# Two parts of 304 and 240 tokens in place of two of 272 in a two-layer encoder step

## The chip, the cores and the metric

One core of one Trainium2 chip runs one program that holds the whole step. The metric is the device time of one execution in microseconds. The kernel before takes 1821.96 us (median of three runs, 1821.05 to 1822.27).

## What is computed

Inference of two layers of a hybrid encoder on 512 prompt frames and 32 frames of a running stream. The reference, cut to what matters here:

```python
a_in, a_gate, u, v, q, k, vv, g = jnp.split(x @ w_in, IN_SPLITS, axis=-1)     # 1024 -> 6656
y_a = silu(layer_norm(causal_dwconv(conv_ext, conv_w, conv_b), ...))          # width 31
y_b = gelu(u) * spatial_gate(layer_norm(gelu(v), ...), sgu_w, sgu_b)
y_c = stick_breaking attention of q, k, vv (8 heads of 64)
merged = sum(sigmoid(g_i + b_gate_i) * (y_i @ w_branch[i]) for the 3 branches)
x = layer_norm(DN_ALPHA * x + merged @ w_out, ln1_g, ln1_b)
f_gate, f_val = jnp.split(x @ w_up, 2, axis=-1)                               # 1024 -> 2 x 2816
f = gelu(causal_dwconv(ffn_ext, ffn_conv_w, ffn_conv_b)) * f_val              # width 3
x = layer_norm(DN_ALPHA * x + f @ w_down, ln2_g, ln2_b)
```

All data is float32. Returned are the new x of all 544 frames and the new rows of the caches and states.

## The kernel before

**Layout.** Features lie on the 128 partitions, the 544 tokens (512 of the prompt, then 32 of the stream) on the free axis. x is `xT[128, 8, 544]`. A matmul takes a 128x128 block of weights as its stationary operand and the tokens as its moving operand. The output bank holds 512 float32 columns, so the tokens are worked on in two parts of `HALF` = 272 columns; `dcol(h)` is the slice of part h. Part 1 holds the last 240 prompt tokens (`BP`) and the 32 of the stream.

**Precision.** Every dense product is made of three matmuls in the type float32r: a weight chunk `raw` is split into a rounded `wh` (ScalarE, `hi`, L495) and the rest `wl` (VectorE, `lo`, L961), the activations likewise into `xh` and `xl`, and `three` (L1628, L1633, L1634) issues wh·xh, wh·xl and wl·xh into one bank. Each of the three loads its own 128x128 block of weights first.

```python
first = mm(out, a, xs[0], start=start, stop=False)
mm(out, a, xs[1], start=False, stop=False)
return mm(out, b, xs[0], start=False, stop=stop)
```

**Units and chunks.** `unit(s, b, ...)` makes one output tile of 128 features for one part: 8 (or 4) times `three`. A chunk of w_in or w_up (2048 columns, 1 MB) gives four units: two feature tiles, each for part 0 (banks 0 and 1) and part 1 (banks 2 and 3). w_branch chunks are half as large. w_out (4 chunks) is worked through for part 0 and, with its chunks kept, for part 1. Per layer that makes 832 calls of `three` for w_in, 192 for w_branch, 128 for w_out, 704 for w_up and 352 for w_down, 2208 in all; half of them are of part 0 and half of part 1.

**The down projection.** `down(h)` runs four times in a layer, twice with part 0 and twice with part 1 (once for output tiles 0 to 3, once for 4 to 7). The 22 input tiles come in groups of 3, 4, 3, 4, 4, 4 (`KGROUPS`), each its own chunk of `raw`; a chunk serves four banks, so one of 4 tiles is 48 matmuls and one of 3 tiles is 36, all of one part.

**The weights' ring.** Three slots. SyncE issues the DMA of a chunk once TensorE has begun the chunk after the last user of the slot (`slot_free`), ScalarE rounds it, VectorE makes the low half, and TensorE waits for that (`lo_full`). Both engines work strictly in the order in which the program lists their instructions, so a `hi` or `lo` behind a step of a norm waits for that step.

**The norms.** `residual`, `shift_sum`, `centre`, `square_first`, `squares_open`, `last_tiles`, `square_last`, `variance`, `off_mean`, `inverse`, `norm`, `norm_out` and `low_tiles` make the LayerNorm of one part while TensorE works on the other; `shift` and `moments` are its matmuls with plain float32 operands, which go as two passes each. The squares of the last four tiles lie in `gex`, pair sums in `cbuf`. The order of all of it is written out by hand per engine. After the last matmul of the program the norm of part 1 has nothing beside it (`tail_tiles`, L1055 to L1098, `y_tile`, L534).

Of the kernel before, what the change touches and what calls it, by code (L numbers as in the profile page):

```python
# [5 lines left out]
F32 = mybir.dt.float32  # L6
# [10 lines left out]
HALF = T // 2  # L17
BP = SEQ - HALF
# [94 lines left out]
def trunk(nc, adds, x_in, win, wbr, wout, wup, wdn, par_in, bc_in, sguw_in, kc_in, vc_in, gh_in, fh_in,  # L113
          y_out, k_out, v_out, glu_out, ffn_out, sgu_out):
    with ExitStack() as ctx:
# [35 lines left out]
        st0 = sb("st0", [P, HALF])  # L151
        st1 = sb("st1", [P, HALF])
        st2 = sb("st2", [P, HALF])
# [3 lines left out]
        tmp = sb("tmp", [P, 4, HALF])  # L157
# [5 lines left out]

        gex = sb("gex", [P, 2, GEX])
        C = top[0]
        cbuf = sb("cbuf", [P, 2, GEX - 2])
# [6 lines left out]
        fhh = [sb(f"fhh{h}", [P, FT, HALF], F32R, at=F + h * 2 * FT * HALF * 4) for h in range(2)]  # L173
        fll = [sb(f"fll{h}", [P, FT, HALF], F32R, at=F + (2 * h + 1) * FT * HALF * 4) for h in range(2)]
# [11 lines left out]
        sq = sb("sq", [P, KT, HALF], at=F + 39168)  # L186
# [12 lines left out]
        sqc = [sb("sqc0", [P, CT, HALF], at=F + 90016), sb("sqc1", [P, CT, HALF], at=F + 71168)]  # L199

        cst = [st0[:, :], cbuf[:, 0, 0:HALF]]
        csd = [st1[:, :], cbuf[:, 0, HALF:2 * HALF]]
        cinv = [st2[:, :], cbuf[:, 1, 0:HALF]]
# [227 lines left out]
        def _(pool):  # L431
# [45 lines left out]
            for t in range(4, KT):  # L477
                x = xT[:, t, dcol(1)]
                g.tensor_tensor(x, x, cbuf[:, 0, 0:HALF], ALU.subtract).then_inc(tail_cent, c.up(tail_cent))
# [3 lines left out]
        def _(act):  # L483
# [19 lines left out]
            def conv_root(h):  # L503
                act.wait_ge(ln_var, c.take(ln_var))
                A(csd[h], cbank[h][:, 0:HALF], ACT.Sqrt, bias=eps[:, 0:1]).then_inc(ln_std, c.up(ln_std))

            def square_first(h):
                act.wait_ge(lx_cent, c.take(lx_cent))
                A(tmp[:, :, :], xT[:, 0:4, dcol(h)], ACT.Square).then_inc(lx_sq, c.up(lx_sq))

            def square_last(h):
                for b in range(4):
                    c.skip(acc_full[b])
                    act.wait_ge(acc_free[b], c.take(acc_free[b]))
                    A(square(b), xT[:, 4 + b, dcol(h)], ACT.Square).then_inc(lx_sq, c.up(lx_sq))

            def root(first=None):
# [3 lines left out]
                A(st2[:, :], bo[:, 0:HALF], ACT.Square).then_inc(lx_msq, c.up(lx_msq))  # L521
                act.wait_ge(lx_var, c.take(lx_var))
                A(st2[:, :], st1[:, :], ACT.Sqrt, bias=eps[:, 0:1]).then_inc(lx_std, c.up(lx_std))

            def norm_out(h, gname, bname, tiles=range(KT)):
                for t in tiles:
# [75 lines left out]
            def plain(dst, m, b, sig_to, fn=ACT.Copy):  # L602
# [3 lines left out]
                A(dst[:, m, dcol(h)], ps[b][:, 0:HALF], fn).then_inc(acc_free[b], c.up(acc_free[b]))  # L606
# [29 lines left out]
            for l in range(DEPTH):  # L636

                def gate(b, t):
                    act.wait_ge(acc_full[b], c.take(acc_full[b]))
                    A(tmp[:, t, :], ps[b][:, 0:HALF], ACT.Sigmoid).then_inc(acc_free[b], c.up(acc_free[b]))  # L640

                def two_gates(b, t):
                    for m in range(2):
                        gate(b + m, t + m)
# [11 lines left out]
                if l == 0:  # L656
                    two_gates(0, 0)
                    two_values(2)
                    two_gates(0, 2)
# [4 lines left out]
                    for b in range(4):  # L664
                        gate(b, b)
                else:
                    root()
                    hi()
                    two_gates(0, 0)
# [4 lines left out]
                    two_gates(0, 0)  # L674
                    two_gates(2, 2)
# [3 lines left out]
                    two_gates(2, 2)  # L679
# [1402 lines left out]
```

## Time and profile before

| | |
|---|---|
| median of 3 runs | 1821.96 us |
| the profiled execution's own time | 1822.0 us |
| its span, first to last instruction | 1820.3 us |
| TensorE matmul busy / weight load busy | 1804.0 us (99%) / 1761.1 us (97%) |
| VectorE, ScalarE, GpSimd busy | 1135.1 us (62%), 771.5 us (42%), 88.9 us (5%) |
| mean granted TensorE clock | 0.997 |
| mean DMA rate | 102 GB/s |

Matmuls are pipelined: each is shown from its start to the landing of its last column, so neighbours overlap, and what the engine really pays for one is the distance between two starts. Weight loads are shown on a row of their own, PEld.

### The profile page before, as it was taken

What the parts mean: (1) busy time and instruction counts of PE and PEld (TensorE: products, weight loads), DVE (VectorE), ACT (ScalarE), POOL (GpSimd) and SP (SyncE); (2) the same over time, 40 slices, a digit from 0 to 9 for tenths busy, and PEclk for the clock granted to TensorE, in tenths of its full rate; (3) what the DMA queues carried; (4) which work ended last, traced back from release to release, by engine and by line L of the source; (5) the groups of instructions that cost most, each with busy time, mean ns of one, the idle gap of its engine ahead of it and who ended that gap; (6) DMA issues with size and microseconds to landing.
All of it is one profiled execution on the core that took longest, in us unless ns stands there. A gap on an engine that the chain in (4) does not pass through costs nothing.

```text
span 1820.3 us, 32909 instructions
## 1 busy us (share of the span) xinstructions
PE 1804.0 (99%) x14362; PEld 1761.1 (97%) x14362; DVE 1135.1 (62%) x1737; ACT 771.5 (42%) x1220; POOL 88.9 (5%) x159
## 2 busy tenths in 40 slices
PE   9999999999999999999999999999999999999997
PEld 9998899999999999999999889999999999999997
DVE  5788677654764444446668886676557644445565
ACT  4245432353553444434542564333544544434343
POOL 0024000000100000000000340000001000000000
PEclk9999999999999999999999999999999999999999
DMA  4521122222222222255525211222232222223544
GB/s 169 190 95 48 36 95 70 82 93 93 95 83 78 93 93 94 68 182 174 170 85 190 75 67 36 72 88 87 82 128 70 72 91 93 93 79 99 182 160 134
DMA packets 36512, 186.02 MB, mean 102 GB/s; under 512 B 7376, under 2 KB 11728, under 8 KB 18192
## 3 DMA queue, kind: packets, MB, share of 16 engines
q1 hardware_dynamic: 34960, 178.37, 29.0%
q10 hardware_dynamic: 1408, 5.54, 0.8%
q8 instruction: 113, 1.85, 0.4%
q14 instruction: 31, 0.25, 0.0%
HBM read 176.75 MB, written 7.15 MB: 101 GB/s over the span
## 4 chain that ended last, share of the span: by engine, by line
PE 95%; DVE 3%; ACT 1%; DMA 1%; issue 0%; ACTq 0%; DVEq 0%
PE acc L1628 29%; PE acc L1633 28%; PE acc L1634 28%; PE score L1702 1%; DVE wl L961 1%; PE small L1750 1%; PE turned L1729 1%; ACT wh L495 1%; DMA raw<-wdn 1%; PE score L1633 1%; PE score L1634 1%; PE score L1628 1%; PE small L1762 1%; PE turned L1786 0%; PE score L1904 0%
## 5 line engine op out<-in xcount | busy, mean ns | idle before, releaser
L1628 PE MATMUL acc<-xh,wh 128*128 128x272 f32 x2944 | 858.7, 292 | 2.5 <-DVE xl L915 1.5
L1633 PE MATMUL acc<-xl,wh 128*128 128x272 f32 x2944 | 848.5, 288 | 0.0
L1634 PE MATMUL acc<-xh,wl 128*128 128x272 f32 x2944 | 847.5, 288 | 0.0
L1628 PEld LDWEIGHTS acc<-xh,wh 128*128 128x128 f32 x2944 | 555.3, 189 | 18.1 <-issue 13.1
L1633 PEld LDWEIGHTS acc<-xl,wh 128*128 128x128 f32 x2944 | 555.0, 189 | 0.1
L1634 PEld LDWEIGHTS acc<-xh,wl 128*128 128x128 f32 x2944 | 553.9, 188 | 0.0
L961 DVE TENSOR_TENSOR wl<-raw,wh 128x2048 fp32r<-128x2048 f32 (+2 forms) x154 | 318.4, 2068 | 204.1 <-ACT wh L495 203.3
L495 ACT ACTIVATE wh<-raw 128x2048 fp32r<-128x2048 f32 (+2 forms) x174 | 304.9, 1753 | 158.9 <-DMA raw<-wdn 112.1
L1628 PE MATMUL acc<-fhh,wh 128*128 128x272 f32 x704 | 204.9, 291 | 1.9 <-DVE wl L961 1.8
L1634 PE MATMUL acc<-fhh,wl 128*128 128x272 f32 x704 | 202.6, 288 | 0.0
L1633 PE MATMUL acc<-fll,wh 128*128 128x272 f32 x704 | 202.6, 288 | 0.0
L1164 DVE SCALAR_TENSOR_TENSOR acc<-glu,par,acc 128x574 f32<-128x574 f32 x240 | 180.8, 813 | 0.1
L1495 DVE SCALAR_TENSOR_TENSOR cbuf<-gex,par,cbuf 128x546 f32<-128x546 f32 x44 | 34.5, 784 | 197.9 <-ACT cbuf L840 197.9
L1628 PEld LDWEIGHTS acc<-fhh,wh 128*128 128x128 f32 x704 | 132.6, 188 | 3.5 <-DVE wl L961 3.1
L1633 PEld LDWEIGHTS acc<-fll,wh 128*128 128x128 f32 x704 | 132.4, 188 | 0.2
L1634 PEld LDWEIGHTS acc<-fhh,wl 128*128 128x128 f32 x704 | 132.4, 188 | 0.0
L746 ACT ACTIVATE tmp<-acc,par 128x272 f32<-128x272 f32 x96 | 46.6, 488 | 198.1 <-PE acc L1634 198.0
L1628 PE MATMUL acc<-mh,wh 128*128 128x272 f32 x256 | 74.9, 293 | 0.0
L1108 DVE TENSOR_TENSOR_SCAN keep<-keep,zero 128x128 f32<-128x128 f32 (+4 forms) x68 | 58.8, 865 | 25.5 <-POOL beta L461 16.9
L1633 PE MATMUL acc<-ml,wh 128*128 128x272 f32 x256 | 73.8, 288 | 0.0
L1634 PE MATMUL acc<-mh,wl 128*128 128x272 f32 x256 | 73.5, 287 | 0.0
L849 ACT ACTIVATE fhh<-tmp 128x272 fp32r<-128x272 f32 x88 | 35.2, 431 | 82.0 <-DVE tmp L1523 42.3
(256 smaller groups left out, 2255.8 us busy)
## 6 DMA issues: line engine op xcount, KB each, us to landing
raw<-win SPq DMA_DIRECT2D x50, 1024.0 KB, 4.9
raw<-wup SPq DMA_DIRECT2D x44, 1024.0 KB, 4.9
raw<-wdn SPq DMA_DIRECT2D x32, 1024.0 KB, 4.9
raw<-wbr SPq DMA_DIRECT2D x24, 512.0 KB, 3.6
raw<-wdn SPq DMA_DIRECT2D x16, 768.0 KB, 4.2
raw<-wout SPq DMA_DIRECT2D x8, 1024.0 KB, 4.9
v_out<-vfm ACTq DMA_DIRECT2D x2, 1088.0 KB, 9.4
k_out<-k ACTq DMA_DIRECT2D x2, 1088.0 KB, 4.7
```

The costliest lines, as they stand in the source:

```text
L495: A(wh[s][:, 0:n], raw[s][:, 0:n], ACT.Copy).then_inc(hi_full[s], c.up(hi_full[s]))
L746: A(tmp[:, b, :], ps[b][:, 0:HALF], ACT.Sigmoid, bias=col(par, PAR["b_gate"] + 8 * BRANCHES[n] + 2 * i + b % 2)).then_inc(acc_free[b], c.u ...
L849: A(row(fhh[b // 2], 2 * i + b % 2, 0, HALF), tmp[:, b, :], ACT.Copy).then_inc(f_hi, c.up(f_hi))
L961: v.tensor_tensor(wl[s][:, 0:n], raw[s][:, 0:n], wh[s][:, 0:n].bitcast(F32), ALU.subtract).then_inc(lo_full[s], c.up(lo_full[s]))
L1108: v.tensor_tensor_scan(keep[b][:, T - w:T][:, ::-1], keep[b][:, T - w:T][:, ::-1], zero[:, 0:1].broadcast_to([P, w]), 1.0, ALU.mult, ALU.a ...
L1164: v.scalar_tensor_tensor(out=acc[:, m, :], in0=glu_at(m, j), scalar=w, in1=acc[:, m, :], op0=ALU.mult, op1=ALU.add).then_inc(vec, c.up(vec))
L1495: v.scalar_tensor_tensor(out=cbuf[:, m, :], in0=gex[:, m, 1:GEX - 1], scalar=col(par, PAR["fw"] + FT + t), in1=cbuf[:, m, :], op0=ALU.mult ...
L1628: first = mm(out, a, xs[0], start=start, stop=False)
L1633: mm(out, a, xs[1], start=False, stop=False)
L1634: return mm(out, b, xs[0], start=False, stop=stop)
L1702: mm(bs[b][:, 0:w], q[rows, ht, i * P:w], k[rows, ht, 0:w], start=True, stop=True).then_inc(s_full[b], c.up(s_full[b]))
L1729: last = pe.transpose(bt[:, kb * P:(kb + 1) * P], beta[n % 2][part][:, kb * P:(kb + 1) * P], ident[:, :])
```

## The change

The parts become 304 and 240 tokens in every stage. Instructions, their order, their number, their waits and the DMAs stay the same; only widths and addresses differ. Part 1 now holds 208 prompt tokens and the 32 of the stream. Buffers of one part's width get the wider one, and the squares and pair sums get places of their own in the room of `gex` and `cbuf`.

```diff
-HALF = T // 2
-BP = SEQ - HALF
+N0, N1 = 304, 240
+PART = (N0, N1)
+WIDE = max(PART)
+BP = SEQ - N0
...
-        st0 = sb("st0", [P, HALF])
+        st0 = sb("st0", [P, WIDE])
...
-        tmp = sb("tmp", [P, 4, HALF])
+        tmp = sb("tmp", [P, 4, WIDE])
...
-        fhh = [sb(f"fhh{h}", [P, FT, HALF], F32R, at=F + h * 2 * FT * HALF * 4) for h in range(2)]
+        f_at = (0, 2 * FT * N0 * 4)
+        fhh = [sb(f"fhh{h}", [P, FT, PART[h]], F32R, at=F + f_at[h]) for h in range(2)]
...
+        squared = [sb(f"squared{b}", [P, WIDE], at=G + o * 4) for b, o in enumerate((8, 552, 856, 1160))]
+        pair = sb("pair", [P, 2, WIDE], at=G + 1464 * 4)
...
         def dcol(h):
-            return slice(h * HALF, (h + 1) * HALF)
-        def square(b):
-            return gex[:, b // 2, 4 + b % 2 * HALF:4 + (b % 2 + 1) * HALF]
+            return slice(h * N0, N0 + h * N1)
+        def square(b, h):
+            return squared[b][:, 0:PART[h]]
...
-                v.tensor_tensor(cbuf[:, 0:2, 0:HALF], x[:, 0:2], x[:, 2:4], ALU.add).then_inc(vec, c.up(vec))
+                v.tensor_tensor(pair[:, :, 0:PART[h]], x[:, 0:2], x[:, 2:4], ALU.add).then_inc(vec, c.up(vec))
...
+                part = b // 2 if h is None else h
                 for t in range(nk):
-                    last = three((spare or ps[b])[:, 0:HALF], s, t * 256 + m * P, [x[:, t, dcol(b // 2 if h is None else h)] for x in xs],
+                    last = three((spare or ps[b])[:, 0:PART[part]], s, t * 256 + m * P, [x[:, t, dcol(part)] for x in xs],
...
-                                last = three(ps[b][:, 0:HALF], s, t * 512 + b * P,
+                                last = three(ps[b][:, 0:PART[h]], s, t * 512 + b * P,
```

Every other operation on one part (gates, products, norms, the loads of x and the stores of y) changes its width in the same way.

## Rows read from the trace of the kernel before

**Rows 1.** The page: span, busy time of the engines, granted clock in 40 slices.
```profile
span 1820.3 us, 32909 instructions
PE 1804.0 (99%) x14362; PEld 1761.1 (97%) x14362; DVE 1135.1 (62%) x1737; ACT 771.5 (42%) x1220; POOL 88.9 (5%) x159
PEclk9999999999999999999999999999999999999999
```

**Rows 2.** The page: the chain that ended last, shares by engine.
```profile
PE 95%; DVE 3%; ACT 1%; DMA 1%; issue 0%; ACTq 0%; DVEq 0%
```

**Rows 3.** Groups by line and form, PE: count, busy us, mean ns, idle before.
```profile
L1628 PE MATMUL acc<-xh,wh 128*128 128x272 f32 x2944 | 858.7, 292 | 2.5 <-DVE xl L915 1.5 <-DVE wl L961 1.0
L1628 PE MATMUL acc<-fhh,wh 128*128 128x272 f32 x704 | 204.9, 291 | 1.9 <-DVE wl L961 1.8
```

**Rows 4.** Busy time by stretch: us, PE busy (count), PEld, DVE, ACT, POOL, clock.
```profile
600.00:700.00 100.00, 100.00 (x800) 100.00 (x799) 45.52 (x94) 40.31 (x68) 0.00 (x0) 1.00 0.24 85
```

**Rows 5.** One line's instructions: duration ns min/median/max, first and last start, forms.
```profile
L1628 PE MATMUL acc<-xh,wh x2944: 282/288/576, 7.3 to 1671.0; 128*128 128x272 f32 x197
L1667 PE MATMUL small<-st,mean_c x16: 390/392/392, 472.9 to 1783.9; 128*128 128x272 f32 x16
L1714 PE MATMUL score<-sfuture,identr x4: 283/283/284, 194.4 to 1099.2; 128*128 128x32 f32 x4
```

**Rows 6.** Timeline, matmuls and weight loads at 272 us: start, us, instruction, count.
```profile
272.36 0.28 PE L1634 MATMUL acc<-xh,wl 128*128 128x272 f32 x1
272.57 0.96 PEld L1896 LDWEIGHTS turned<-wsgu,ntok 32*128 32x128 f32 x8
272.57 1.07 PE L1896 MATMUL turned<-wsgu,ntok 32*128 32x32 f32 x8
273.57 1.19 PEld L1904 LDWEIGHTS score<-wsgu,ntok 128*128 128x128 f32 x10
```

**Rows 7.** Waits of PE, longest first: us in total, times, longest.
```profile
PE acc L1628 <- DVE wl L961: 2.8, 7, 0.6
```

**Rows 8.** The page: DMA issues of w_down's chunks, us from issue to landing.
```profile
raw<-wdn SPq DMA_DIRECT2D x32, 1024.0 KB, 4.9
```

**Rows 9.** Timelines of ACT, DVE and PE in the last layer's down projection.
```profile
1739.28 1.90 ACT L495 ACTIVATE wh<-raw 128x2048 fp32r<-128x2048 f32 x1
1741.21 2.29 DVE L961 TENSOR_TENSOR wl<-raw,wh 128x2048 fp32r<-128x2048 f32 x1 [0.93 <-ACT wh L495]
1743.56 0.39 PE L1628 MATMUL acc<-fhh,wh 128*128 128x272 f32 x1 [0.61 <-DVE wl L961]
...
1788.76 1.28 DVE L1011 TENSOR_TENSOR xT<-xT,small 128x1088 f32<-128x1088 f32 x1
1790.08 1.11 ACT L509 ACTIVATE tmp<-xT 128x1088 f32<-128x1088 f32 x1 [4.75 <-DVE xT L1011]
1791.10 1.90 ACT L495 ACTIVATE wh<-raw 128x2048 fp32r<-128x2048 f32 x1
1793.03 2.29 DVE L961 TENSOR_TENSOR wl<-raw,wh 128x2048 fp32r<-128x2048 f32 x1 [2.99 <-ACT wh L495]
1795.38 0.39 PE L1628 MATMUL acc<-fhh,wh 128*128 128x272 f32 x1 [0.56 <-DVE wl L961]
```

**Rows 10.** Timeline of the tail after the last matmul of a product.
```profile
1807.73 0.44 DVE L1055 TENSOR_TENSOR xT<-xT,acc 128x272 f32<-128x272 f32 x1 [0.24 <-PE acc L1634]
1809.41 0.73 DVE L1077 TENSOR_TENSOR xT<-xT,cbuf 128x544 f32<-128x544 f32 x1 [0.77 <-ACT cbuf L901]
1811.26 1.84 DVE L1081 RECIPROCAL st<-st 128x272 f32<-128x272 f32 x1
1813.99 3.48 ACT L534 ACTIVATE xT<-sq,par 128x272 f32<-128x272 f32 x6 [2.95 <-DVE sq L1086]
```

**Rows 11.** Timeline of the head: the low half of a piece of x.
```profile
9.68 0.73 DVE L915 TENSOR_TENSOR xl<-xT,xh 128x544 fp32r<-128x544 f32 x1
```

More of the change, by code:

```diff
@@ L162, in trunk @@
         rs = sb("rs", [P, 2, 5])
+        G = top[0]
         gex = sb("gex", [P, 2, GEX])
         C = top[0]
+        assert C == G + 2 * GEX * 4
         cbuf = sb("cbuf", [P, 2, GEX - 2])
@@ L172, in trunk @@
         wl.append(sb("wl3", [P, CHUNK], F32R, at=F + 71168))
-        fhh = [sb(f"fhh{h}", [P, FT, HALF], F32R, at=F + h * 2 * FT * HALF * 4) for h in range(2)]
-        fll = [sb(f"fll{h}", [P, FT, HALF], F32R, at=F + (2 * h + 1) * FT * HALF * 4) for h in range(2)]
+        f_at = (0, 2 * FT * N0 * 4)
+        fhh = [sb(f"fhh{h}", [P, FT, PART[h]], F32R, at=F + f_at[h]) for h in range(2)]
+        fll = [sb(f"fll{h}", [P, FT, PART[h]], F32R, at=F + f_at[h] + FT * PART[h] * 4) for h in range(2)]
         yb = [sb(n, [P, CT, T], F32R, at=F + i * T4) for i, n in enumerate(("ybh", "ybl"))]
@@ L198, in trunk @@
         att = [sb("att0", [P, 5 * P], at=S), sb("att1", [P, 5 * P], at=M)]
[L199 to L203, printed above, removed]
+        sqc = [sb("sqc0", [P, CT, N0], at=F + 90016), sb("sqc1", [P, CT, N1], at=F + 71168)]
+        cst = [st0[:, 0:N0], cbuf[:, 0, 0:N1]]
+        csd = [st1[:, 0:N0], cbuf[:, 0, N1:2 * N1]]
+        cinv = [st2[:, 0:N0], cbuf[:, 1, 0:N1]]
+        squared = [sb(f"squared{b}", [P, WIDE], at=G + o * 4) for b, o in enumerate((8, 552, 856, 1160))]
+        pair = sb("pair", [P, 2, WIDE], at=G + 1464 * 4)
+        assert 552 >= GEX + 2 and 8 + WIDE <= GEX and 1464 + 2 * WIDE <= 2 * GEX + 2 * (GEX - 2)
         ps = [ctx.enter_context(nc.psum_tensor(f"acc{b}", [P, 512], F32)) for b in range(4)]
@@ L478, in _ @@
                 x = xT[:, t, dcol(1)]
-                g.tensor_tensor(x, x, cbuf[:, 0, 0:HALF], ALU.subtract).then_inc(tail_cent, c.up(tail_cent))
+                g.tensor_tensor(x, x, pair[:, 0, 0:N1], ALU.subtract).then_inc(tail_cent, c.up(tail_cent))
         @block.scalar
@@ L514, in square_last, with root @@
                     act.wait_ge(acc_free[b], c.take(acc_free[b]))
-                    A(square(b), xT[:, 4 + b, dcol(h)], ACT.Square).then_inc(lx_sq, c.up(lx_sq))
-            def root(first=None):
+                    A(square(b, h), xT[:, 4 + b, dcol(h)], ACT.Square).then_inc(lx_sq, c.up(lx_sq))
+            def root(h, first=None):
                 act.wait_ge(lx_mean, c.take(lx_mean))
@@ L673, in _ @@
                     taken(2)
-                    two_gates(0, 0)
-                    two_gates(2, 2)
+                    two_gates(0, 0, 0)
+                    two_gates(2, 2, 1)
                     hi()
@@ L885, in _ @@
                 his(3)
-                root()
+                root(0)
                 his(2)
@@ L900, in _ @@
                 hi()
-            root(lambda: A(cbuf[:, 0, 0:HALF], bo[:, 0:HALF], ACT.Copy).then_inc(mean_copied, 1))
+            root(1, lambda: A(pair[:, 0, 0:N1], bo[:, 0:N1], ACT.Copy).then_inc(mean_copied, 1))
             for t in (0, 2, 3, 4, 6, 7):
@@ L1596, in _ @@
             dve.wait_ge(mean_copied, 1)
-            off_mean(1, 0, cbuf[:, 0, 0:HALF])
-            variance()
-            off_mean(1, 1, cbuf[:, 0, 0:HALF])
-            inverse()
+            off_mean(1, 0, pair[:, 0])
+            variance(1)
+            off_mean(1, 1, pair[:, 0])
+            inverse(1)
             for p in range(4):
@@ L1677, in conv_means @@
                     pe.wait_ge(ln_sum, c.take(ln_sum))
-                    mm(cbank[h][:, 0:HALF], mean_c[:, :], cst[h], start=True, stop=True).then_inc(ln_mean, c.up(ln_mean))
+                    mm(cbank[h][:, 0:PART[h]], mean_c[:, :], cst[h], start=True, stop=True).then_inc(ln_mean, c.up(ln_mean))
             def conv_vars():
@@ L1682, in conv_vars @@
                     pe.wait_ge(ln_ssum, c.take(ln_ssum))
-                    mm(cbank[h][:, 0:HALF], mean_c[:, :], cst[h], start=True, stop=True).then_inc(ln_var, c.up(ln_var))
+                    mm(cbank[h][:, 0:PART[h]], mean_c[:, :], cst[h], start=True, stop=True).then_inc(ln_var, c.up(ln_var))
             qk_out = {}
@@ L1814, in _ @@
                         for b in range(2):
-                            last = three(ps[b][:, 0:HALF], s0, t * 256 + b * P, [x[:, t, dcol(0)] for x in xs],
+                            last = three(ps[b][:, 0:N0], s0, t * 256 + b * P, [x[:, t, dcol(0)] for x in xs],
                                          t == 0, t == KT - 1)
```

211 lines of the change are left out of this document (105 added, 106 removed).

## The prediction

> **What bounds the kernel now.** I read the page first: matmuls are in flight 99% of a span of 1820.3 us, VectorE is busy 62%, ScalarE 42%, and the granted clock is full in all 40 slices [rows 1], which is the 2.4 GHz level. The chain that ended last runs through PE for 95% of the span [rows 2]. So the time is a number of matmuls times the distance between two starts, plus the few places where PE waits. By form [rows 3] nearly everything is 272 columns wide and PE hardly sat idle before them. The code gives the count: 2208 calls of `three` in a layer, so 3 x 2208 x 2 = 13,248 matmuls, 6624 of each part.
>
> The distance comes from the table of stretches: 800 matmuls touch 100 us of the up projection [rows 4]. Each counts over its own 0.288 us [rows 5], so it is (100 + 0.29)/800 = 125.4 ns. 13,248 x 0.1254 = 1661 us of 1820. The question is what these 125.4 ns are made of: columns, or the weight load that goes beside each.
>
> **The price of a column.** 272 columns at 2.4 GHz are 113.3 ns. The float32 passes (L1667) take two clocks a column, 226.7 ns, and last 392 ns from start to landing, so the way through the array is 392 - 227 = 165 ns. The float32r matmuls last 288 ns [rows 5]; less 165 that is 123 ns in which 272 columns stream, and 2.4 ns between two streams make the 125.4. They stream 8% slower than the clock allows. This isn't the next weight load's doing: the matmul at 272.36 lasts 0.28 too, and the next load starts only at 272.57, behind its stream [rows 6]. I take the 123 ns as proportional to columns: 304 cost 137.5 + 2.4 = 139.9 ns, 240 cost 108.5 + 2.4 = 110.9 ns, together 250.8 as before. If the excess were fixed per matmul they would be 138.7 and 112.1, the same sum. A straight line gives nothing and costs nothing here, and I see no term that bends down.
>
> **The price of a load.** The eight matmuls of L1896 have 32 columns, so their loads set the pace: 0.96 us for eight, less one load's 0.19, over seven is 110 ns. The ten loads of L1904 give (1.19 - 0.19)/9 = 111 ns [rows 6]. A load can't be had faster than about 111 ns, and a narrow matmul needs 110.9. Before, the load was hidden with 14 ns to spare; now the two tie. With equal means the later one sets each step: the durations of float32r matmuls scatter from 282 ns up around 288 [rows 5], some +-3 ns usually. Taking the larger of 111.5 and a value scattering by 2.5 about 111 gives some 112.4. **+1.5 ns x 6624 = +9.9 us.** Bounds: 0 if the load hides at 108 or so (the tie never bites), +5 ns (+33 us) if load and stream disturb each other's start at a tie. I take 1.5, nearest to the load rows, measured at that pace.
>
> The Trainium skill ("TensorE: Matmul & The Clock Gate", sections "LDWEIGHTS (loading the stationary operand)" and "Back-to-back issue gap") gives a load P/1.2, so 107 ns for 128 columns, and a matmul N/2.4 + 2.5 ns. By it the narrow part would be paced by its loads at 106.7 instead of 102.5, the wide one would take 129.2, the pair 4.3 ns more than 2 x 115.8, and an estimate from that page is +28 us. The trace has 125.4 where that rule has 115.8, so I go by the rows.
>
> **Weights in `down`.** A part is one operand of a whole chunk there. With part 1 a chunk of four input tiles takes 48 x 0.1124 = 5.4 instead of 6.0 us, one of three tiles 4.05 instead of 4.5; with part 0 they take 6.7 and 5.0. The weights come at the same pace: 4.9 us to land [rows 8], 1.9 rounding, 2.3 low half [rows 9], 9.1 in all, while two chunks run. Two chunks are now 10.5 or 12.0 us; with part 1 they are 9.5 or 10.8, so it still just fits where nobody is held up. It is held up twice in a layer. Behind `square_last(0)` ScalarE starts a chunk at 1739.28, VectorE at 1741.21, PE at 1743.56 [rows 9]: that chain hangs on the end of part 0 and is not shortened, PE's work over it (one chunk of three) is 0.45 us shorter. Behind `centre(1)` and `square_first(1)` (to 1791.10) PE starts at 1795.38: here two chunks, 1.1 us of PE's work, go against 0.4 us that the narrower norm saves. So the waits grow by 0.45 + 0.7 us; twice, since both layers do it, but in layer 0 the second wait is short now: **+2.2 us**. Bounds 0 and +6 (three more stalls of 0.5 to 1 us where a landing is late). All waits for low halves are 2.8 us now [rows 7].
>
> **The ends.** After the last product the norm of part 1 is alone [rows 10]. Widths fall by 12%: the reciprocal 1.84 x 32/272 = 0.21 us, three passes over two tiles 0.07 each, the others with the last `y` tiles 0.2: **-0.6 us**. The head does the reverse: a piece of x is 12% wider, 0.07 us on each pass [rows 11] and up to 0.4 us of landing: **+0.3 us**. The float32 passes of the norms cost two clocks a column, a straight line again. VectorE and ScalarE have slack in every other stage. New addresses of squares and pair sums change no instruction and no wait. The norm of part 0 behind w_out grows by some 0.8 us and its cover shrinks from 24.1 to 21.6 us; its low tiles are done 2.5 us ahead now and wait for the residual of tile 5 in any case, so nothing.
>
> Sum: 9.9 + 2.2 - 0.6 + 0.3 = +11.8 us on the profiled execution's own 1822.0, which is the median (1821.96). **1834 us.**
>
> **Rivals.** *The load stays hidden* (not slower). Place: every narrow matmul; it decides if the load's own pace is below 110.9 ns. Then the first term is 0, the second about half (streams end a bit earlier, waits too), and 1822 + 1 = 1823 us. For it: my two load paces are 110 and 111, on the edge. Against: a tie leaves no room. 15%.
>
> *The load is the pace already.* The 12 ns above column time come with the load: then the narrow matmul takes 111 + 10 = 121 ns (+10 x 6624 = +66 us, 1888) or even the full 125.4 (+14.5, 1918). Against: the stream of 123 ns without a load beside it [rows 6]. 9%.
>
> *Half rate for a narrow operand.* If under some width float32r went at two clocks a column as float32 does, 240 would take 202 ns: +91 x 6624 = +603 us, 2425. Against: L1714 has 32 columns and lands after 283 ns [rows 5]; a load of 110, 13 of columns and 165 make 288, two clocks a column would make 301. 3%.
>
> *Slack found elsewhere* (faster). The tail and every wait for low halves go: -0.6 - 2.8 and part of the seams, 1817 us. Against: waits in `down` hang on part 1, which gets less cover. 5%.
>
> **How the numbers follow.** My forecast holds 68%. A measurement of this kernel can tell about 0.2%, 3.6 us, from no change. Faster is the last rival with the best of the hidden load: 0.07. Within 3.6 us lies the hidden load and the low edge of the forecast: 0.18. The rest is slower: 0.75. The range goes from 1821, where the load hides and only the ends change, to 1860, where the bound of 5 ns and the stalls meet; the forecast's own range is 1826 to 1850. Outside stay the loaded pace, the half rate and most of the faster case.
>
> **What would show it.** Stretches of the up projection should hold as many matmuls as now within 1%. Starts of 304 columns 139 to 140 ns apart, of 240 columns 112 to 113, with the narrow ones lasting more than 273 ns where they wait for a load. PE's wait for low halves grows to some 5 us, all with part 1 of `down`. I am wrong if narrow starts are 111 apart or less (the first rival), above 116 (the second), or if the wide ones aren't near 139.9: then a column's price isn't what I took.

## The result, and the profile after

The kernel after takes 1836.78 us (median of six runs, 1834.4 to 1839.37); the kernel before, in six runs beside it, 1822.02 (1821.05 to 1822.59). The ratio is 1.008, 95% interval 1.007 to 1.0091: slower by 0.8%. The profiled execution took 1838.0 us; its span is 1836.3, 16.0 more than the 1820.3 of [rows 1], and these 16.0 us are what is taken apart below. Among the runs below, one execution of the reordered kernel at 304 and 240 took 4605.63 us and one at 284 and 260 took 2519.14; the ratios leave these two out.

The page of the kernel after, header, busy time and the chain's shares:

```profile
span 1836.3 us, 32909 instructions
PE 1812.3 (99%) x14362; PEld 1768.9 (96%) x14362; DVE 1137.0 (62%) x1737; ACT 771.3 (42%) x1220; POOL 91.0 (5%) x159
PE 93%; DVE 4%; ACT 2%; DMA 1%; issue 0%; ACTq 0%; DVEq 0%
```

The same instructions as in [rows 1, 2], and VectorE's and ScalarE's busy time barely moved. The chain leaves PE more often: 93% where it was 95%. The forms on PE (columns as in [rows 3]; the three matmuls of `three` are now L1637, L1642 and L1643):

```profile
L1637 PE MATMUL acc<-xh,wh 128*128 128x304 f32 x1504 | 460.0, 306 | 4.9 <-DVE wl L970 2.6 <-DVE xl L924 2.3
L1637 PE MATMUL acc<-xh,wh 128*128 128x240 f32 x1440 | 400.1, 278 | 0.0
```

A matmul of 272 lasted 288 ns [rows 5]. Now a wide one lasts 302 (306 on this line, whose mean holds the restarts after a wait) and a narrow one about 274. The distance between two starts can be read in the timeline, PE alone, where narrow matmuls give way to wide ones:

```profile
640.53 0.27 PE L1637 MATMUL acc<-xh,wh 128*128 128x240 f32 x1
640.64 0.27 PE L1642 MATMUL acc<-xl,wh 128*128 128x240 f32 x1
640.75 0.27 PE L1643 MATMUL acc<-xh,wl 128*128 128x240 f32 x1
640.86 0.30 PE L1637 MATMUL acc<-xh,wh 128*128 128x304 f32 x1
641.00 0.30 PE L1642 MATMUL acc<-xl,wh 128*128 128x304 f32 x1
641.14 0.30 PE L1643 MATMUL acc<-xh,wl 128*128 128x304 f32 x1
```

0.11 us for 240 columns, 0.14 for 304. Over all starts in the trace that follow one another without a stall the means of these products are **112.15 and 139.85 ns, where 272 columns took 125.41**. A pair costs 252.0 instead of 250.8, +1.18 ns, and 6624 pairs make **+7.8 us**. The stretch of [rows 4] shows how little that is: 799 matmuls instead of 800.

```profile
600.00:700.00 100.00, 100.00 (x799) 100.00 (x798) 46.99 (x93) 40.29 (x67) 0.00 (x0) 1.00 0.24 85
```

Most of the rest of the 16 us is waits. Those of PE by releaser (in total, times, longest), beside [rows 7]:

```profile
PE acc L1637 <- DVE wl L970: 8.1, 8, 1.6
PE acc L1637 <- DVE xT L1446: 2.4, 1, 2.4
```

The 2.8 us for low halves became 8.1, and a wait for a residual, 2.4 us long, is new. The longer ones of the eight in the timeline, with what goes ahead of the last two (the wait stands in brackets):

```profile
326.55 0.41 PE L1637 MATMUL acc<-xh,wh 128*128 128x304 f32 x1 [0.65 <-DVE wl L970]
...
853.69 0.38 PE L1637 MATMUL acc<-fhh,wh 128*128 128x240 f32 x1 [1.16 <-DVE wl L970]
...
906.23 0.38 PE L1637 MATMUL acc<-fhh,wh 128*128 128x240 f32 x1 [1.58 <-DVE wl L970]
...
1760.27 1.90 ACT L506 ACTIVATE wh<-raw 128x2048 fp32r<-128x2048 f32 x1
1762.21 2.29 DVE L970 TENSOR_TENSOR wl<-raw,wh 128x2048 fp32r<-128x2048 f32 x1 [0.86 <-ACT wh L506]
1764.55 0.38 PE L1637 MATMUL acc<-fhh,wh 128*128 128x240 f32 x1 [1.16 <-DVE wl L970]
...
1796.69 10.38 SPq L340 DMA_DIRECT2D raw<-wdn  x3
1802.04 1.91 ACT L506 ACTIVATE wh<-raw 128x2048 fp32r<-128x2048 f32 x1 [3.87 <-DMA raw<-wdn]
1809.35 1.89 ACT L506 ACTIVATE wh<-raw 128x2048 fp32r<-128x2048 f32 x1
1811.28 2.29 DVE L970 TENSOR_TENSOR wl<-raw,wh 128x2048 fp32r<-128x2048 f32 x1 [2.87 <-ACT wh L506]
1813.63 0.38 PE L1637 MATMUL acc<-fhh,wh 128*128 128x240 f32 x1 [1.64 <-DVE wl L970]
```

The first stands for four (326.55, 383.67, 1237.42, 1294.55): seams between a branch and the next, 0.25 us each before. The others lie in `down` with part 1; 1764.55 and 1813.63 answer to the two of [rows 9], 0.61 and 0.56 there. A w_down chunk still lands in 4.9 us, as in [rows 8]. A stall costs more than its bracket: at 326.55 the bracket says 0.65 us, and the distance of the two starts was 925 ns where 112 are usual (537 at this place before, with a bracket of 0.25). Counted by the distance of the starts instead of the bracket, all stalls for low halves, a few short ones included, grew by **5.4 us**.

The new wait is in layer 0, in the second `down` with part 1 (timeline, the rows that matter):

```profile
880.84 0.28 PE L1643 MATMUL acc<-fhh,wl 128*128 128x240 f32 x1
...
881.91 0.62 ACT L542 ACTIVATE xh<-sq,par 128x304 fp32r<-128x304 f32 x1
...
882.57 0.47 DVE L1102 TENSOR_TENSOR xl<-xT,xh 128x304 fp32r<-128x304 f32 x1 [0.59 <-ACT xh L542]
882.96 1.34 DVE L1446 SCALAR_TENSOR_TENSOR xT<-xT,acc 128x240 f32<-128x240 f32 x4
...
883.50 0.35 PE L1637 MATMUL acc<-fhh,wh 128*128 128x240 f32 x1 [2.39 <-DVE xT L1446]
...
886.22 0.41 PE L1643 MATMUL acc<-fhh,wl 128*128 128x240 f32 x1
```

`down(1)` has filled its four banks and must have them emptied by `residual(b, b, 1)`, L1446. On VectorE this stands behind `low_tiles(0, range(4, KT))`, which follows ScalarE's `norm_out` of part 0 tile by tile, 16 passes of 304 columns. Both sides moved the wrong way: the norm got wider, the work over it narrower. **+2.4 us.** The last row is the second half of the matter: right behind the wait the matmuls last 0.41 us. By stretch (columns as in [rows 4]):

```profile
884.70:888.10 3.40, 3.40 (x18) 3.40 (x17) 3.00 (x3) 0.00 (x0) 0.00 (x0) 0.51 0.70 231
888.50:892.00 3.50, 3.50 (x34) 3.50 (x33) 1.73 (x1) 1.49 (x1) 0.00 (x0) 1.00 0.42 105
```

3.4 us at the lower of TensorE's two levels, a granted clock of 0.51, which is 1.2 GHz, then full again: 18 matmuls, where a stretch 0.1 us longer holds 34 at full clock, **+1.7 us**. Away from the two ends the execution before had one such stretch, at 1109 us; the one after had that one (1120) and this.

The tail, beside [rows 10]:

```profile
1822.09 0.40 DVE L1065 TENSOR_TENSOR xT<-xT,acc 128x240 f32<-128x240 f32 x1 [0.95 <-PE acc L1643]
...
1827.94 1.64 DVE L1091 RECIPROCAL st<-st 128x240 f32<-128x240 f32 x1
...
1830.41 3.21 ACT L545 ACTIVATE xT<-sq,par 128x240 f32<-128x240 f32 x6 [2.61 <-DVE sq L1096]
```

From the start of the last product's matmul to the end it takes 11.9 us instead of 12.9: **-1.0**. The sum is 7.8 + 5.4 + 2.4 + 1.7 - 1.0 = 16.3 us for the 16.0 measured. The 1.7 us needn't come with the change: the six executions after had mean granted clocks from 0.996 (1838.03 and 1839.37 us) to 0.999 (1834.4 us), and the profiled one is among the two lowest. Without this term the sum is 14.6, beside the 14.8 us between the medians.

### The profile page after: what moved, and what is told of

Its sections match the earlier page's. It is cut to its first block, busy times and chain, and to the rows that moved or that the text cites. A ratio compares the mean times of both kernels' runs of the same rounds, so it can differ in the third digit from the quotient of the medians.

```text
span 1836.3 us, 32909 instructions
## 1 busy us (share of the span) xinstructions
PE 1812.3 (99%) x14362; PEld 1768.9 (96%) x14362; DVE 1137.0 (62%) x1737; ACT 771.3 (42%) x1220; POOL 91.0 (5%) x159
## 3 DMA queue, kind: packets, MB, share of 16 engines
q1 hardware_dynamic: 34960, 178.31, 28.7%
## 4 chain that ended last, share of the span: by engine, by line
PE 93%; DVE 4%; ACT 2%; DMA 1%; issue 0%; ACTq 0%; DVEq 0%
PE acc L1637 28%; PE acc L1642 28%; PE acc L1643 28%; DVE wl L970 2%; PE score L1712 1%; PE small L1760 1%; PE turned L1739 1%; DMA raw<-wdn 1%; ACT wh L506 1%; PE score L1637 1%; PE score L1642 1%; PE score L1643 1%; PE small L1772 1%; PE turned L1796 0%; PE score L1914 0%
## 5 line engine op out<-in xcount | busy, mean ns | idle before, releaser
L1637 PE MATMUL acc<-xh,wh 128*128 128x240 f32 (+1 forms) x2944 | 860.1, 292 | 4.9 <-DVE wl L970 2.6
L1642 PE MATMUL acc<-xl,wh 128*128 128x240 f32 (+1 forms) x2944 | 851.5, 289 | 0.0
L1643 PE MATMUL acc<-xh,wl 128*128 128x240 f32 (+1 forms) x2944 | 848.5, 288 | 0.0
L1637 PEld LDWEIGHTS acc<-xh,wh 128*128 128x128 f32 x2944 | 555.0, 189 | 20.4 <-issue 14.9
L1642 PEld LDWEIGHTS acc<-xl,wh 128*128 128x128 f32 x2944 | 556.3, 189 | 0.0
L1643 PEld LDWEIGHTS acc<-xh,wl 128*128 128x128 f32 x2944 | 555.0, 189 | 0.0
L1637 PE MATMUL acc<-fhh,wh 128*128 128x240 f32 (+1 forms) x704 | 206.4, 293 | 8.0 <-DVE wl L970 5.5
L1642 PE MATMUL acc<-fll,wh 128*128 128x240 f32 (+1 forms) x704 | 204.1, 290 | 0.0
L1643 PE MATMUL acc<-fhh,wl 128*128 128x240 f32 (+1 forms) x704 | 203.7, 289 | 0.0
L1637 PEld LDWEIGHTS acc<-fhh,wh 128*128 128x128 f32 x704 | 133.6, 190 | 10.4 <-DVE wl L970 7.1
L1642 PEld LDWEIGHTS acc<-fll,wh 128*128 128x128 f32 x704 | 133.5, 190 | 0.3
L1643 PEld LDWEIGHTS acc<-fhh,wl 128*128 128x128 f32 x704 | 133.6, 190 | 0.0
L757 ACT ACTIVATE tmp<-acc,par 128x304 f32<-128x304 f32 (+1 forms) x96 | 46.7, 488 | 198.3 <-PE acc L1643 198.2
L1637 PE MATMUL acc<-mh,wh 128*128 128x304 f32 (+1 forms) x256 | 75.1, 293 | 0.0
L1642 PE MATMUL acc<-ml,wh 128*128 128x304 f32 (+1 forms) x256 | 73.9, 289 | 0.0
L1643 PE MATMUL acc<-mh,wl 128*128 128x304 f32 (+1 forms) x256 | 73.5, 287 | 0.0
```

What stands on the lines that cost most here:

```text
L757: A(tmp[:, b, 0:PART[b // 2]], ps[b][:, 0:PART[b // 2]], ACT.Sigmoid, bias=col(par, PAR["b_gate"] + 8 * BRANCHES[n] + 2 * i + b % 2)).then ...
```

## The experiments

Ratios are to the kernel before, run beside each. The expectations call the theories by letters; A is the one of the prediction, by which a narrow matmul pays because its stream and the next load tie. The line numbers in `three` shift by a few with each kernel.

**What a width costs by itself.** The kernel before, with rows of 96 products of one width put behind its last matmul, into a bank that nobody reads any more.

```diff
+            pe.wait_ge(acc_free[0], c.seen(acc_free[0]))
+            for width in (272, 304, 272, 256, 248, 240, 232, 224, 192, 128, 64):
+                for i in range(96):
+                    mm(ps[0][:, 0:width], wh[i % 2][:, i % 16 * P:(i % 16 + 1) * P],
+                       (xh, xl)[i % 3 % 2][:, i % KT, 0:width], start=True, stop=True)
```

> The kernel before, and behind its last matmul eleven rows of 96 float32r matmuls each, with 128x128 weights of their own and 272, 304, 272, 256, 248, 240, 232, 224, 192, 128 and 64 columns. Theory A (a matmul costs the later of its columns, 0.452 ns each + 2.4 ns, and of its weight load, about 111.5 ns): 125.4 ns from start to start at 272 columns, 139.9 at 304, 118 at 256, 114.5 to 115 at 248, 112 to 112.5 at 240, and 111 to 112 flat for every width from 232 down to 64. Theory B (no floor, a straight line): 110.9 at 240, 103.7 at 224, 89 at 192, 60 at 128. Theory C (load and columns disturb each other near a tie): a bump of 3 ns or more over A between 232 and 256, gone at 192. Theory D (a narrow operand goes at half rate): 200 ns or more under some width.

The timeline of PE, the second matmul of each row of products; 96 distances lie between two of these lines:

```profile
1821.56 0.30 PE L2013 MATMUL acc<-xl,wh 128*128 128x304 f32 x1
...
1834.99 0.29 PE L2013 MATMUL acc<-xl,wh 128*128 128x272 f32 x1
...
1846.98 0.28 PE L2013 MATMUL acc<-xl,wh 128*128 128x256 f32 x1
...
1869.44 0.28 PE L2013 MATMUL acc<-xl,wh 128*128 128x240 f32 x1
...
1880.19 0.27 PE L2013 MATMUL acc<-xl,wh 128*128 128x232 f32 x1
...
1890.91 0.27 PE L2013 MATMUL acc<-xl,wh 128*128 128x224 f32 x1
```

304 columns: (1834.99 - 1821.56)/96 = 139.9 ns; 272: 11.99/96 = 124.9; 240: 10.75/96 = 112.0; 232: 10.72/96 = 111.7. Between them 256 took 118.8 and 248 115.3; below, 224, 192 and 128 all took 111.7. Most of the row of 64 ran at a granted clock of 0.5, so it says nothing here. So the load's own pace is 111.7 ns and the knee lies between 240 and 232, under the narrow part. There is no bump where the two meet: 256, 248 and 240 lie on one line, 8 columns a step of 3.4 ns. The sweep gives both widths of the kernel (139.9 and 112.0 against 139.85 and 112.15). It also points at the dear one: in clocks of 2.4 GHz above one a column, 240 pays 28.7, 272 pays 28.0 and 304 pays 32.0.

**The layout alone**, with both parts 272 again.

```diff
-N0, N1 = 304, 240
+N0, N1 = 272, 272
```

> The changed kernel with both parts at 272: only the new places of the squares and pair sums are left of the change. My theory: they change no instruction and no wait, ratio to the kernel before 0.999 to 1.001, about 1822 us. Rival: the new places cost or give something (other banks, a wait), ratio off by over 0.001, in which case that share of the 14.8 us isn't the widths'.

1822.03 us, ratio 0.9995 (0.9986 to 1.0004), span 1820.3, the waits as before. The new places of squares and pair sums cost nothing; all of the change is in the widths.

**The residual ahead of the low tiles**, to take the new wait away.

```diff
-                    low_tiles(0, range(4, KT))
                 for b in range(4):
                     residual(b, b, 1)
+                if not final:
+                    low_tiles(0, range(4, KT))
```

> The changed kernel (304 and 240), but in layer 0 VectorE takes the four residuals of part 1 before the low halves of part 0's tiles 4 to 7, which ScalarE's norm delivers late. If the wait of 2.5 us for xT (L1446) and the half clock behind it come from that order, both go: 1836.8 - 2.5 - 1.5 = about 1833 us, with the next wait for a low half (1.9 us in layer 0) perhaps smaller too, down to 1831. Rival: ScalarE is the late one and holds up the weights behind the norm anyway; then the wait only moves on to the next chunk and the time stays within 1 us of 1836.8.

1835.89 us, ratio 1.0069 (1.0056 to 1.0081). The wait for the residual is gone, and another took its place, as the rival in the expectation had it (waits of PE, then ScalarE, VectorE and PE in the timeline):

```profile
PE acc L1638 <- DVE wl L970: 9.4, 9, 1.6
```

```profile
882.55 1.90 ACT L506 ACTIVATE wh<-raw 128x2048 fp32r<-128x2048 f32 x1
...
884.48 2.29 DVE L970 TENSOR_TENSOR wl<-raw,wh 128x2048 fp32r<-128x2048 f32 x1 [0.28 <-ACT wh L506]
...
886.83 0.38 PE L1638 MATMUL acc<-fhh,wh 128*128 128x240 f32 x1 [1.60 <-DVE wl L970]
```

ScalarE rounds the next chunk only behind `norm_out`, from 882.55 on; its low half starts at 884.48, and PE waits 1.60 us for it. The clock didn't fall behind this wait. The wait isn't VectorE's order alone: the late thing is ScalarE's norm of part 0, and what is queued behind it on either engine.

**Less unequal parts**, 288 and 256.

```diff
-N0, N1 = 304, 240
+N0, N1 = 288, 256
```

> The changed kernel with parts of 288 and 256. Theory A (load as a floor under the narrow part): both widths are on the line, 132.6 + 118.1 = 250.7 ns a pair, nothing lost in the matmuls; waits in the down projection grow by half of what 240 did, 1 to 3 us, the tail gives 0.3 to 0.5: 1822 to 1826 us. Rival (the loss grows with the difference of the parts): half of the 14.8 us, so 1829 us.

1832.23 us, ratio 1.0049 (1.0036 to 1.0061). This is what upset theory A, which wanted 1822 to 1826: here a narrow matmul is 7 ns clear of the load, and the pair still costs as much as at 304 and 240. The rival of the expectation, half of the loss and so 1829, missed it too. In the kernel 288 columns take 133.15 ns, 256 take 118.94, together 252.1. Only the waits are smaller:

```profile
PE acc L1637 <- DVE wl L970: 5.4, 8, 1.2
PE acc L1637 <- DVE xT L1446: 1.1, 1, 1.1
```

The start distances in clocks of 2.4 GHz say where the price lies. 272 columns take 301.0 clocks, 29 more than columns; 240 take 269.2, also 29 more; 304 take 335.6, 31.6 more; 288 take 31.6 and 256 take 29.5 more. **The narrow part pays just what 272 pays. The wide one pays 2.6 clocks more**, 1.1 ns a pair.

These are means over operands in different places, and the place has a price too. In the kernel before, where all are 272 wide, products of the high halves of the branches' outputs start 124.4 ns apart in part 0 and 127.5 in part 1. To see the width alone, take only the products of x in part 0, which start at column 0 of each tile in every kernel: they pay 27.4 clocks above columns at 256, 29.7 at 272, 33.4 at 284, 31.5 at 288 and 32.0 at 304 (256 and 284 from runs further down). So the wide part's price stands with the place kept.

**The price by width, finely.** As the first sweep, other widths, some of them starting at another column.

```diff
+            rows_ = [(w_, 0) for w_ in (272, 264, 268, 272, 274, 276, 278, 280, 284, 288, 296, 304, 320, 384, 512)]
+            rows_ += [(272, 272), (272, 4), (280, 264), (304, 240), (240, 304)]
```

> The kernel before, with twenty rows of 96 float32r matmuls behind its last one, most of them between 264 and 304 columns, five of them starting at another column of the operand. The first row of widths (e1) put the loss not where I had forecast it: 240 to 256 columns lie on one line of 1/2.4 ns a column plus 12 ns (112, 115.3, 118.8), 304 columns lie 1.3 ns above that line. Theory A' (a width above 272 pays a step): 264 and 268 on the line of the narrow ones (122.1, 123.8), 272 at 125.0 to 125.4, and a jump of 1 to 1.5 ns at one width between 273 and 288, then 1/2.4 ns a column again up to 512 (about 226.7 there). Rival A'' (a price that grows with columns): no jump, 0.45 ns a column through the whole row, 512 at 235 or more. Rival P (the place of the operand, not its width): rows of one width that start at column 4, 240, 264, 272 or 304 differ by over 1 ns from those that start at 0; by A' they agree within 0.5.

```profile
1844.37 0.29 PE L2015 MATMUL acc<-xl,wh 128*128 128x272 f32 x1
...
1856.22 0.29 PE L2015 MATMUL acc<-xl,wh 128*128 128x274 f32 x1
...
1905.25 0.29 PE L2015 MATMUL acc<-xl,wh 128*128 128x284 f32 x1
...
1917.75 0.30 PE L2015 MATMUL acc<-xl,wh 128*128 128x288 f32 x1
...
1930.54 0.30 PE L2015 MATMUL acc<-xl,wh 128*128 128x296 f32 x1
...
1988.09 0.39 PE L2015 MATMUL acc<-xl,wh 128*128 128x512 f32 x1
...
2010.06 0.29 PE L2015 MATMUL acc<-xl,wh 128*128 128x272 f32 x1
```

In this stretch 272 columns took 11.85/96 = 123.4 ns, 284 took 12.50/96 = 130.2, 288 took 12.79/96 = 133.2, 512 took 21.97/96 = 228.9 (230.0 within the row, without the step to the next). So four columns from 284 to 288 cost 3.0 ns where the clock asks 1.7. Clocks above columns, from the means of all starts of a row:

| columns | clocks above columns |
|---|---|
| 264, 276, 280, 284 | 28 |
| 272: first row, second row, from column 4 on, from column 272 on | 28, 24, 24, 32 |
| 268, 274, 278 | 30 to 32 |
| 288, 296, 304, 320 | 32 |
| 384 | 36 |
| 512 | 40 |

The price above columns goes up with the width, mostly in steps of four clocks (1.7 ns), and isn't a matter of the width alone: 304 columns from column 240 on took 29, from column 0 on 32; 280 from column 264 on took 31, from 0 on 28; 272 stands at 24, 28 and 32. A bare count of columns doesn't tell it.

**The norm's low tiles spread out**, both orders of the third experiment put right at once.

```diff
                     hi()
-                    norm_out(0, "ln2_g", "ln2_b", range(4, KT))
+                    norm_out(0, "ln2_g", "ln2_b", range(4, 6))
+                    hi()
+                    norm_out(0, "ln2_g", "ln2_b", range(6, KT))
...
-                his(3)
+                his(3 if final else 2)
...
-                    low_tiles(0, range(4, KT))
                 for b in range(4):
                     residual(b, b, 1)
                 shift_sum(1)
+                if not final:
+                    lo()
+                    low_tiles(0, range(4, KT))
-                los(3)
+                los(3 if final else 2)
```

> As e3, and in layer 0 ScalarE takes one chunk's rounding between tiles 5 and 6 of part 0's norm, VectorE one chunk's low half before part 0's tiles 4 to 7. e3's trace shows TensorE at 885 us waiting 1.9 us for a low half whose rounding stood behind eight steps of the norm on ScalarE. If the order on ScalarE is the cause, this wait goes nearly all, 1.5 to 2 us less than e3, so 1833 to 1834.5 us, and no half clock in that place. Rival: the chunk had landed late, the wait stays, 1836.

1833.57 us, ratio 1.0062 (1.0048 to 1.0075), as expected. The wait at 880 us is gone with nothing in its place; what is left are the waits of the other stages:

```profile
PE acc L1641 <- DVE wl L972: 8.3, 9, 1.6
```

**The load as the pace inside the kernel**: parts of 320 and 224, below the knee.

```diff
-N0, N1 = 304, 240
+N0, N1 = 320, 224
...
-        squared = [sb(f"squared{b}", [P, WIDE], at=G + o * 4) for b, o in enumerate((8, 552, 856, 1160))]
-        pair = sb("pair", [P, 2, WIDE], at=G + 1464 * 4)
+        squared = [sb(f"squared{b}", [P, WIDE], at=G + o * 4) for b, o in enumerate((8, 552, 872, 1192))]
+        pair = sb("pair", [P, 2, WIDE], at=G + 1512 * 4)
```

> The changed kernel with parts of 320 and 224. By the row of widths in e1 a matmul of 224 columns can't start sooner than 111.7 ns after the last, and 320 columns are 1/2.4 ns each above 304's 140.0, so 146.7: 258.4 ns a pair, +7.6 x 6624 = +50 us in the matmuls. Waits for weights grow beside part 1 (+8 to +15 us over the kernel before) and the tail gives 1: 1822 + 50 + 11 - 1 = about 1882 us. Rival (no floor in the kernel itself, loads pulled ahead further): 252 ns a pair, 1822 + 8 + 11 = 1841 us.

1879.8 us, ratio 1.0318 (1.0304 to 1.0332). Here the stretch shows it plainly, 777 matmuls where there were 799:

```profile
600.00:700.00 100.00, 100.00 (x777) 100.00 (x776) 44.46 (x88) 39.05 (x64) 0.00 (x0) 1.00 0.24 85
```

224 columns take 111.96 ns, where the line of the wider ones (29 clocks above columns) would give 105; 320 take 146.48. The pair costs 258.4, 7.6 ns more than before, 50.5 us in all. So the floor of the prediction is real. It lies just below 240, and the change stopped right above it.

**The wide part last**, 256 and 288: if the waits come from a wide norm of part 0 over narrow work of part 1, they should be small here.

```diff
-N0, N1 = 304, 240
+N0, N1 = 256, 288
...
-        sq = sb("sq", [P, KT, WIDE], at=F + 39168)
+        sq = sb("sq", [P, KT, WIDE], at=F + 34816)
...
-        csd = [st1[:, 0:N0], cbuf[:, 0, N1:2 * N1]]
-        cinv = [st2[:, 0:N0], cbuf[:, 1, 0:N1]]
+        csd = [st1[:, 0:N0], cbuf[:, 1, 0:N1]]
+        cinv = [st2[:, 0:N0], gex[:, 1, 0:N1]]
```

> Parts of 256 and 288, the narrow one first: the mirror of e4, the same matmuls in another order (a buffer of the norms, sq, moved to make room). The matmuls cost what they cost in e4, 252.1 ns a pair, +8.5 us. If the rest of the loss is waits beside the narrow part 1 (low halves behind its short units, the down projection's chunks), they shrink instead of growing: the four waits at 327, 384, 1232 and 1289 us go from 0.54 to 0.3 us or less, those of the down projection's second half from 0.9 to 0.6; the tail is 0.3 us longer. 1822 + 8.5 - 1.5 + 0.3 = 1829 us, 3 less than e4. Rival (any unequal split costs these waits, whichever part is narrow): 1832 us as e4.

1827.34 us, ratio 1.0028 (1.0017 to 1.004), 4.9 us under its mirror image (1829 was expected). In this kernel one buffer of part 1 overwrites the zero history of the width-3 convolution, so the first outputs of that convolution start from other values; no time hangs on that. The last run repeats it with the history left alone.

**A better order at 272**, from what the waits taught: in `down` one more chunk is rounded ahead of `square_first`, in `down(0)` another ahead of the last square (`between`), with its low half ahead of the last sum (`late`); at the seams between branches the low half goes in behind the product of the first bank instead of the second.

```diff
-                his(3)
+                his(4)
                 square_first(0)
-                his(3)
-                square_last(0)
-                his(3)
+                his(2)
+                square_last(0, hi)
+                his(2)
...
-                his(3)
+                his(4)
                 square_first(1)
-                his(3)
+                his(2)
...
-                        if b == 1 and n < 2:
-                            if n == 0:
-                                lo_second()
-                            else:
-                                lo()
+                        if b == 1 and n == 0:
+                            lo_second()
+                        if b == 0 and n == 1:
+                            lo()
...
-                last_tiles(0)
-                los(3)
+                last_tiles(0, None, lo)
+                los(2)
```

> The kernel before with four waits for low halves taken away by order alone: in the second branch VectorE makes the next chunk's low half after the first product instead of after the second; in the down projection one chunk is rounded before the last square of part 0 and one before square_first of either part, and its low half made before the last sum of squares. If those waits are a matter of order, they go (4 x 0.41 at 325, 382, 1226 and 1282 us, 0.77 at 842 and 1743, 0.73, 0.26 and 0.17 at 1795, 1726 and 894): 4.3 us, 1818 us, ratio 0.9976. Rival: the DMA is the late one or the wait moves to the next chunk, ratio 0.999 or more.

1816.9 us, ratio **0.9968** (0.9956 to 0.9979): faster than both kernels. Its five executions all had a granted clock of 0.998; beside those of the kernel before at 0.998 the gain is 4.4 us, which is nearer to the 4.3 expected than the 5.1 between the medians. Of the waits of PE for low halves none is left, and one of 0.3 us for a residual is new; the longest now:

```profile
PE acc L1631 <- DVE xl L917: 1.5, 1, 1.5
PE turned L1797 <- POOL mean_d L437: 1.1, 1, 1.1
```

**The same order at 304 and 240**, together with the spread low tiles.

> e6 (304 and 240) with the same reordering as e9. It takes away all the loss that is waits and leaves what the widths cost in the matmuls (1.2 ns a pair, +7.8 us) less the shorter tail (-1): against e9 (about 1818 us) +7 us, so 1825 us, ratio to the kernel before 1.0015. Rival (the waits in the down projection are supply, two short chunks against 9.1 us of DMA, rounding and low half): they stay in part, 1828 to 1831 us.

1823.95 us, ratio 1.0011 (1.0002 to 1.002). PE waits longest in sum for `xl` at the head, 1.6 us in two; for low halves 0.1 us is left. This kernel and the last one differ in the widths and in the low tiles' order, and the waits that order could take away are gone in both: 1823.95 - 1816.9 = 7.05 us, where 7.8 for the pairs less 1.0 for the tail make 6.8. The spans of the two profiles are 8.5 us apart, of which 1.7 are a stretch at a granted clock of 0.5 that only this one has (211 us), and 6.8 remain. So the price of the widths stands nearly by itself, and the other 7.7 us of the 14.8 were the order of two queues that no longer fitted. The weights came no faster here, so it wasn't their supply (the rival of the expectation).

**Where the step lies**: parts of 284 and 260.

```diff
-N0, N1 = 304, 240
+N0, N1 = 284, 260
```

> Parts of 284 and 260. In e5 the price above one clock a column was 28 clocks at 264 to 284 columns and 32 from 288 to 320, so the step sits between 284 and 288. If it sits there in this kernel too, a pair costs what 272 twice do (250.8 ns) and only the waits beside part 1 are left: 1822 + 2.5 = about 1825 us, 6 to 7 us less than e4 with 4 columns more on the wide side. Rival (the price depends on the operand's place as much as on its width, as e5's rows at columns 240, 264 and 272 hint): starting part 1 at column 284 costs some clocks more, 1828 to 1832 us.

1830.99 us, ratio 1.0044 (1.0031 to 1.0057): the rival's range, not the 1825 expected. 284 columns took 131.73 ns, 260 took 120.03; +0.94 ns a pair, 6.2 us. The sweep's 28 clocks for 284 didn't hold here: the mean is 32. Nor was it one figure: 132.2 ns where the tokens come from x, 130.6 where they come from anything else (f, the branches' outputs and their sum). So the place of the operand counts beside its width.

**The wide part last, with the zero history kept.**

```diff
-N0, N1 = 304, 240
+N0, N1 = 256, 288
...
-        sq = sb("sq", [P, KT, WIDE], at=F + 39168)
+        sq = sb("sq", [P, KT, WIDE], at=F + 34816)
...
-        csd = [st1[:, 0:N0], cbuf[:, 0, N1:2 * N1]]
-        cinv = [st2[:, 0:N0], cbuf[:, 1, 0:N1]]
+        csd = [st1[:, 0:N0], cbuf[:, 1, 0:N1]]
+        cinv = [st2[:, 0:N0], gex[:, 1, 4:4 + N1]]
```

> e8 with the inverse deviations of part 1's conv norm kept 4 columns further on, clear of the zeros that stand ahead of the width-3 convolution; nothing that costs time differs. 1827.3 us and a ratio of 1.003 again, 118.5 and 133.2 ns from start to start; off by over 2 us would say that e8's place of that buffer mattered.

1827.24 us, ratio 1.0025 (1.0015 to 1.0036), as its twin. Waits for low halves are 2.1 us, less than before the change, the one for the residual is gone. The cost of unequal parts is then the pairs (133.23 + 118.40, +0.8 ns x 6624 = 5.4 us) and a tail 0.4 us longer (13.3).

## Why the prediction was right, and where it wasn't

The forecast was 1834.0 (range 1821 to 1860), measured 1836.78: slower, as forecast, and 11.8 us became 14.8 in the medians. That the total came so near was partly luck, for the errors have opposite signs: the matmuls were put 2.1 us too high, for a reason that didn't hold, and the waits 5.6 too low (2.2 against 3.7 + 1.6 + 2.4, and 0.1 of short ones). Step by step:

- **Count and distance** of the matmuls: right, 125.4 ns and 13,248.
- **The price of a column** was taken as proportional, 8% over the clock. It isn't: 240 columns cost 112.15 ns, not 110.9, which is 272's price less 32 clocks. What is paid above columns is nearly fixed, 29 clocks, and steps up on the wide side. I had held the two readings to give "the same sum", and with a fixed price exactly 29 they would. The Trainium skill ("TensorE: Matmul & The Clock Gate", section "Back-to-back issue gap") has a fixed 2.5 ns above N/2.4 for a matmul by itself; nearly fixed is the right shape, but the rows have 12 ns at 272 columns and 17 at 512.
- **The tie with the load, +9.9 us**: this step failed. Its size was near (7.8), its place wrong. Load pace and narrow stream do nearly meet (111.7 and 112.15), but a narrow matmul pays nothing for it: 256 and 248 lie on the same line, and 288 with 256, far from the tie, costs the same pair. The extra is paid by the wide matmul. I had taken "the later of two that scatter" for a mechanism, with no row in which the two met. My test ("240: 112 to 113 ns") couldn't tell the two apart, since a fixed price gives 112.1 as well; the wide one's 139.85 fitted my 139.9 by chance.
- **The load's pace**: read as 110 to 111 from eight and ten loads [rows 6], measured 111.7. It stays the reason why no part should go under 240, as the run at 320 and 224 shows.
- **Waits in `down`, +2.2 us**: the mechanism was right, the size too small. The wait behind `square_last(0)` grew by 0.54 in each layer (forecast 0.45), the one behind `square_first(1)` in the last layer by 1.06 (forecast 0.7). The 0.4 us I credited to the narrower norm were there: from ScalarE's 1802.04 to PE's 1813.63 it takes 11.59 us, before 11.97 [rows 9, for its end]. But the landing at the head of it came 0.5 us later against PE's work, since its DMA is issued when PE begins the chunk before (1796.69), and that chunk is shorter too. And its counterpart in layer 0, which I took for short, grew by 1.56. Together 3.7 instead of 2.2.
- **"VectorE and ScalarE have slack in every other stage"**: this step failed too. Four seams between branches grew by 0.39 us each, 1.6 in all: there VectorE's low half stands behind two products of the wide part, and the end of the chunk in front of it is narrow. I had read the sum of [rows 7], not its seven places.
- **The norm of part 0 in `down(1)` of layer 0** isn't in the prediction at all: 2.4 us, and in this execution 1.7 of lower clock behind it. I had looked at the norm behind w_out (where nothing happened, as said) and not at the same norm behind w_down.
- **The ends**: tail -1.0 (forecast -0.6), head 0 (forecast +0.3). The layout: nothing, as said.
- **The rivals**: the hidden load (1823) had the place right, nothing at the narrow matmul, and would have come true but for the wide one's price and the waits. The load as the pace already at 240: no, and where it is the pace, at 224 columns, a matmul takes 112 ns, not the 121 or 125.4 of that rival. Half rate: no width from 128 columns up showed it.

Shown by runs: the layout's zero, the floor, the pair's price at five splits, the wide part's higher price with the place kept, the waits as order (the two tuned kernels), the part that ScalarE's queue has in the new wait. Not settled: why the price above columns goes in steps of four clocks, exactly where it steps, and how the place of an operand enters. No run moved one operand by itself inside the kernel. That the lower clock at 885 us follows from the wait ahead of it isn't shown either. For it: the clock fell 1.2 us behind the end of that wait of 2.4 us, and just so in the run at 320 and 224 behind one of 2.6. It didn't fall behind the 1.6 us in the same place of the third experiment, nor behind the 1.1 us at 288 and 256.

## What to carry to other kernels

When work in two parts is made unequal, don't stop at "the sum is the same": each part is the cover of the other's vector work, so list every place where PE starts a part's product with little to spare, and see which part covers which. Here the parts also had a floor (the next weight load) under the narrow one and a dearer step above the wide one, so equal parts were the best of the splits tried. And read the waits of a kernel one by one before changing widths: the seven small ones, 2.8 us together, told where the change would hurt, and a new order of a few instructions that takes them away is worth 0.3%, where every unequal split lost. The reordered kernel with the wide part last wasn't tried.

## What the runs showed of the hardware beyond that

- A float32r matmul with a weight load beside it costs a nearly fixed 12 ns above its columns (in the sweeps 24 to 32 clocks from 240 to 320 columns), 36 clocks at 384 and 40 at 512, in steps of about four. The same 272 columns took 123.3, 125.0 and 126.6 ns at different places.
- The pace of 128x128 float32r weight loads is 111.7 ns, whatever the width beside it from 128 to 232 columns. The Trainium skill ("TensorE: Matmul & The Clock Gate", section "LDWEIGHTS (loading the stationary operand)") gives P/1.2, by which it would be 106.7; the rows have 5 ns more.
- TensorE's granted clock fell to 0.5 (1.2 GHz) for 3.4 us in the middle of the program, some 1.7 us lost each time. Twelve of these falls, in eleven profiles, come while TensorE is busy without a gap, all at the end of the attention's products in one of the two layers (211 to 218 us, 1108 to 1146 us), right behind 24 or more products with 32 columns of tokens (`small<-att,vc`, L1762 in the kernel before). Two more came behind the waits named above (885 us after, 907 us at 320 and 224), and three of the profiles had none. The falls go with the differences between executions of one kernel: those of the kernel before took 1823.7 us in the mean at a granted clock of 0.996, 1822.2 at 0.997, 1820.6 at 0.998 and 1820.4 at 0.999. What decides whether the clock falls at such a place, no run tested.
